# PEER layer of a hybrid trunk: buffer clear moved into the seventh head, v ring begun at free buffers, samples' join in halves

## The reference, cut to what matters

```python
def _peer(x, w_q, k1, k2, u, v):          # 8 heads, 128 x 128 product keys, top 16
    q = (xb @ w_q).reshape(blk, PEER_HEADS, PEER_KEY_DIM)
    s1, s2 = ...                          # q against both halves of the keys
    e = ...                               # the 16 best of the pairs: expert numbers
    gate = jax.nn.softmax(sv, axis=-1)
    act = jax.nn.gelu(jnp.einsum('thkd,td->thk', u[e], xb).astype(jnp.float32), approximate=False)
    return jnp.einsum('thk,thkd->td', (gate * act).astype(x.dtype), v[e])
x = _layernorm(DEEPNORM_ALPHA * x + h, ln_g[l, 0], ln_b[l, 0])   # h: the mixer
f = _peer(x, ...)
x = _layernorm(DEEPNORM_ALPHA * x + f, ln_g[l, 1], ln_b[l, 1])
```

## Time and profile before

| | us |
|---|---|
| three runs, median | 2099.04 (2098.5 to 2102.95) |
| the profiled execution | 2098.57 |
| its span | 2096.8 |

### The profile page before, as it was taken

One profiled execution on the slowest core, in us unless ns is written; L12 is line 12 of the kernel. 1 busy time (PEld: TensorE's weight loads), 2 busy tenths in 40 slices (PEclk: granted clock), 3 DMA queues, 4 the chain that ended last, 5 costly groups with the idle time before them and its releaser, 6 DMA issues.

```text
span 2096.8 us, 21267 instructions
## 1 busy us (share of the span) xinstructions
PE 1222.8 (58%) x6582; PEld 647.7 (31%) x6582; DVE 1186.6 (57%) x3085; ACT 330.7 (16%) x771; POOL 1196.9 (57%) x1104
## 2 busy tenths in 40 slices
PE   6889778910644566575647736664854433333565
PEld 6667535700112222232214314542432100000111
DVE  3555443997667566666441267889457666664101
ACT  3333221110010222232103002321100000000000
POOL 0111002665777777777764554657367777776675
PEclk9899888965775778798669877876978665565578
DMA  8423033877999999999999998888589999998998
GB/s 280 123 81 103 24 131 121 333 261 296 352 420 411 411 354 407 412 409 410 402 421 347 387 369 298 279 296 305 222 347 419 378 377 384 380 383 331 370 419 337
DMA packets 240392, 670.55 MB, mean 320 GB/s; under 512 B 21241, under 2 KB 94482, under 8 KB 236322
## 3 DMA queue, kind: packets, MB, share of 16 engines
q0 software_dynamic: 152064, 553.72, 68.3%
q1 hardware_dynamic: 85922, 98.82, 13.6%
q10 hardware_dynamic: 2304, 16.78, 2.0%
HBM read 663.12 MB, written 6.10 MB: 319 GB/s over the span
## 4 chain that ended last, share of the span: by engine, by line
POOL 31%; PE 18%; DVE 15%; DMA 14%; issue 13%; DVEq 3%; ACT 3%; SPq 1%; ACTq 1%; PEldq 0%; POOLq 0%; PEld 0%
POOL arena L890 31%; DMA arena<-in_peer_v,idxT 8%; DVE arena L1581 7%; DMA arena<-in_peer_u,idx 5%; PE bank L1070 4%; PE bank L664 3%; PE bank L332 2%; PE bank L987 2%; DVEq L470 2%; PE bank L321 1%; PE bank L384 1%; DMA scratch<-in_cache_kv 1%; PE bank L1081 1%; ACT scratch L421 1%; DVE scratch L529 0%
## 5 line engine op out<-in xcount | busy, mean ns | idle before, releaser
L1581 DVE SCALAR_TENSOR_TENSOR arena<-arena,x 128x1024 f32<-128x1024 f32 x512 | 612.6, 1225 | 329.8 <-DMA arena<-in_peer_u,idx 320.9
L890 POOL DMA_INDIRECT arena<-in_peer_u,idx x512 | 583.6, 1140 | 268.6 <-issue 143.6
L890 POOL DMA_INDIRECT arena<-in_peer_v,idxT x512 | 541.1, 1057 | 258.1 <-issue 143.6
L1070 PE MATMUL bank<-arena,wbig 128*32 128x512 f32 x2048 | 378.8, 874 | 502.1 <-DMA arena<-in_peer_v,idxT 493.8
L1070 PEld LDWEIGHTS bank<-arena,wbig 128*32 128x32 f32 x2048 | 77.4, 138 | 736.7 <-issue 727.5
L468 POOL TENSOR_TENSOR scratch<-scratch 128x128 f32<-128x128 f32 x16 | 7.1, 441 | 200.0 <-DVEq L517 200.0
L687 DVE BATCH_NORM_STATS2 stats<-bank 128x6 f32<-128x512 f32 (+1 forms) x24 | 15.5, 685 | 181.4 <-PEq L1084 85.3
L321 PE MATMUL bank<-xT,arena 128*128 128x264 f32 x512 | 115.3, 386 | 0.6 <-DMA arena<-in_hgrn_w_in 0.6
L321 PEld LDWEIGHTS bank<-xT,arena 128*128 128x128 f32 x512 | 96.7, 190 | 16.8 <-issue 0.7
L2069 PE MATMUL bank<-cst,scratch 128*128 128x128 f32 x192 | 48.0, 353 | 53.7 <-DMA scratch<-in_cache_kv 47.5
L987 PE MATMUL bank<-xT,arena 128*128 128x264 f32 (+2 forms) x352 | 71.5, 366 | 2.8 <-ACT xT L639 2.6
(11 more groups left out here) (408 smaller groups left out, 1879.9 us busy)
## 6 DMA issues: line engine op xcount, KB each, us to landing
arena<-in_hgrn_w_in SPq DMA_DIRECT2D x32, 512.0 KB, 6.0
scratch<-in_peer_w_q ACTq DMA_DIRECT2D x14, 1024.0 KB, 8.5
scratch<-in_cache_kv SPq DMA_DIRECT2D x96, 144.0 KB, 8.6
arena<-in_peer_w_q SPq DMA_DIRECT2D x8, 1024.0 KB, 9.0
arena<-in_peer_u,idx POOLq DMA_INDIRECT x512, 7.4
arena<-in_peer_v,idxT POOLq DMA_INDIRECT x512, 7.7
scratch<-in_mla_w_uq SPq DMA_DIRECT2D x2, 2304.0 KB, 13.0
g_all<-in_cache_kv SPq DMA_DIRECT2D x32, 144.0 KB, 12.3
```

The costliest lines, as they stand in the source:

```text
L890: pool.indirect_dma_start(out=dst, out_offset=None, in_=table, in_offset=bass.IndirectOffsetOnAxis(ap=rows, axis=0)).then_inc(done, 16)
L1070: mm = pe.matmul(ybank(t, c, P, 2 * l + 1)[32 * j:32 * j + 32, :], wspread[q % NQ8][:, j, m, :], slot(row[j][0])[:, 512 * c:512 * c + 512] ...
L1581: dve.scalar_tensor_tensor(slot(r), slot(r), 1.0, x[:, t, :], ALU.mult, ALU.mult, accum_out=dots[t][:, TOPK * h + k:TOPK * h + k + 1]).the ...
```

## The change

1. GpSimd clears the weights' buffer at n = 6, k = 8, after `mixed` 2. The wait for the samples' y stands at v row 4, the wait for the stores at v row 0.
2. The v ring of layer 1 begins at slot 12 instead of 8, and `LAG[1]` is 29 instead of 28: a v row follows u by 116 instead of 112.
3. The samples' join uses banks 2 and 3, waits until tile 1's LayerNorm has read them, and is split: between its halves stand tile 1's turn and head 0's projection and score for tile 1 alone. The turned weights of pairs 0 to 2 come ahead of it.
4. The samples' turn and their part of head 0 come after round 0, heads 1 and 2 after rounds 0 and 1, the spread after round 1, and heads 3 to 7 two rounds later than before.
5. VectorE does tile 1's LayerNorm after the last dots of n = 6 and places the weights at once; the samples' LayerNorm and the route of head 8 move into n = 7. ScalarE follows the new order.

```diff
...
                 return bank[5 + c][0:nt, :]
+            if seq == 2 and t == 2:
+                t = 1
...
                 return 6, 7
-            return (0, 1) if t == 1 or (seq, t) in ((4, 2), (5, 2)) else (2, 3)
+            return (0, 1) if t == 1 or (seq, t) == (4, 2) else (2, 3)
...
                 pe.wait_ge(turn_taken, turned((1, 4)[seq], t))
+                if seq and t == 2:
+                    pe.wait_ge(y_free, normed(2, 1))
...
         SAMPLES_AT = 56
-        LAG = (17, 28)
+        LAG = (17, 29)
         STEP0 = (0, 35)
-        SAMPLE_STEP = (34, 35 + 48)
+        SAMPLE_STEP = (34, 35 + 50)
...
             if l:
-                return STEP0[1] + 24 * rest + 3 * h + s
+                return STEP0[1] + 24 * rest + 3 * h + s + (2 if rest and h else 0)
...
             if l:
-                return STEP0[1] + 24 * t + 3 * h + 2
+                return STEP0[1] + 24 * t + 3 * h + 2 + (2 if t and h else 0)
...
             return 6 + 4 * (h - 1) + 2 + t
+
+        def first_sample_step(s):
+
+            return STEP0[1] + 27 + s
...
             if n < WIDE[l]:
-                return RING + n % RING
-            return (RING + (n - WIDE[l]) % (12, 16)[l]) % (2 * RING)
+                return RING + (n + 4 * l) % RING
+            return (RING + 4 * l + (n - WIDE[l]) % (12, 16)[l]) % (2 * RING)
...
                     for k in range(TOPK):
+                        if l and n == 6 and k == 8:
+                            pool.wait_ge(mixed, 2)
+                            pool.memset(wflat[:, 0:4096], 0.0).then_inc(spread_zero, 1)
...
                         place = TOPK * n + k - 4 * LAG[l]
+                        if l and place == 0:
+                            pool.wait_ge(stored, 96)
+                        elif l and place == 4:
+                            pool.wait_ge(y_ready, normed(2, 2))
...
                 pool.memset(zq, 0.0).then_inc(zq_ready, 1)
-                heads(0, HH - 1)
-                pool.wait_ge(y_ready, normed(2, 2))
-                pool.wait_ge(stored, 96)
-                pool.memset(wflat[:, 0:4096], 0.0).then_inc(spread_zero, 1)
-                heads(HH - 1, 2 * HH)
+                heads(0, 2 * HH)
...
             mm.then_inc(rs_ready, 1)
+
+        def pe_first_samples(pe):
+            for s in range(2):
+                b = pe_step(pe, first_sample_step(s))
+                w = wq1_at(HH)
+                for k in range(KO):
+                    mm = pe.matmul(b[:, 0:NS], w[:, k, s * P:(s + 1) * P], xT[:, k, 2 * P:NT], start=(k == 0), stop=(k == KO - 1))
+                mm.then_inc(rs_ready, 1)
...
             pe_join(pe, 1, 1)
-            pe.wait_ge(idxT_ready, 3 * NQ8)
-            pe_join(pe, 1, 2)
-            pe_turn(pe, 5, 1)
-            pe_turn(pe, 5, 2)
-            pe.wait_ge(turn_taken, turned(5, 2))
-            for h in range(3):
-                ask(h, True)
-                pe_score(pe, 1, h, 1)
-            pe_spread_samples(pe, 1)
...
                 turn_weights(pe, 1, q, 4, 0)
+            pe_join_turn(pe, 1, 2)
+            pe_join_half(pe, 1, 2, 0)
+            pe_turn(pe, 5, 1)
+            pe.wait_ge(turn_taken, turned(5, 1))
+            for s in range(2):
+                pe_project(pe, 1, 0, s, P, 2 * P, True)
+            pe_score(pe, 1, 0, 1)
+            pe_join_half(pe, 1, 2, 1)
...
                 add_round(pe, 1, r)
-                h, j = divmod(r + 6, 2)
-                if h < HH:
+                if r == 0:
+                    pe_turn(pe, 5, 2)
+                    pe.wait_ge(turn_taken, turned(5, 2))
+                    pe_first_samples(pe)
+                if r < 2:
+                    ask(r + 1, True)
+                    pe_score(pe, 1, r + 1, 1)
+                if r == 1:
+                    pe_spread_samples(pe, 1)
+                h, j = divmod(r + 4, 2)
+                if 3 <= h < HH:
...
                     turn_weights(pe, 1, q - 1, q, q - 1)
-                if r == 10:
+                if r == 12:
...
                 if h == 0 and s == 0:
-                    act.wait_ge(zq_ready, l + 1)
+                    act.wait_ge(zq_ready, 1)
...
             ins.then_inc(rs_taken, 1)
+
+        def act_first_samples(act):
+            act.wait_ge(zq_ready, 2)
+            for s in range(2):
+                m = first_sample_step(s)
+                act.wait_ge(rs_ready, m + 1)
+                act.activation(zq[:, s, 0, 0:NS], step_bank(m)[:, 0:NS], ACT.Copy).then_inc(rs_taken, 1)
...
             act_turn(act, 4, 2)
-            act_ln(act, 2, (1, 2))
+            act_ln(act, 2, (1,))
             act_turn(act, 5, 1)
+            for s in range(2):
+                act_query(act, 1, 0, s, P, 2 * P, True)
+            act_score(act, 1, 0, 1)
+            act_ln(act, 2, (2,))
             act_turn(act, 5, 2)
-            for h in range(3):
+            act_first_samples(act)
+            act_load_query(act, HH + 2)
+            for h in range(1, 3):
...
                     q = n // 2
-                    own = n + 2 if n < 6 or 9 <= n < 2 * HH - 2 else 8 if n == 7 else None
+                    own = n + 2 if n < 6 or 9 <= n < 2 * HH - 2 else None
...
                     elif n == 7:
-                        for p in range(3):
-                            place_weights(p)
+                        dve_ln(dve, 2, (2,))
+                        route_keys(8)
...
                     dot(n, 2)
-                    if n == 6:
-                        dve_ln(dve, 2, (1,))
+                    if n == 7:
+                        route_pairs(8)
+                        route_experts(8)
...
                         route_experts(own)
-                    if n % 2 and own and n != 7:
+                    if n % 2 and own:
...
                     elif n == 6:
-                        dve_ln(dve, 2, (2,))
+                        dve_ln(dve, 2, (1,))
+                        for p in range(3):
+                            place_weights(p)
...
```

## The result

| | before, us | after, us |
|---|---|---|
| four runs each, median | 2099.92 (2098.5 to 2102.95) | 2132.39 (2129.07 to 2138.92) |
| span of the profiled execution | 2096.8 | 2127.4 |

The account below looks back on a forecast made before the run. No engine is full; holes in GpSimd's order before 1600 us (24.3 and 16.97) are paid in full. Terms -1.9 + 1.0 - 1.0 + 5.0 + 3.7 = +6.8 on 2098.57 or 2099.04 gave 2105.5 us, range 2090 to 2116.

Parts of the forecast that it names:

- (a): GpSimd's clear ahead of u 104: takes 3.67 us beside dots, so u 104 goes out at 1455.7, +2.7.
- (c): Samples' join on TensorE, waiting for banks 2 and 3: ends at 1503.5 (before 1488.3), with 2.5 added for the clock.
- rival 3: TensorE's clock stays at 1.2 GHz through both join halves and the projection: join 8 to 10 later, 2114, chance 0.12.
- (d): GpSimd during the join: v 4 waits until 1503.8, a hole of 18.6 us; the hole at v 8 closes.
- (f): VectorE's weigh(3) waits for pair 3's gelu behind head 4's score: u 140 at 1581.4, hole some 25 us, 1.9 gain left.
- (g): After u 140: +1.0 at u 144, -1.0 for pace to u 255, +5.0 for lagged gathers, +3.7 for the samples' repack.
- (e): u 128, waiting for head 8's route: out at 1525.4, 26.1 us earlier, with u 123 landing in 7.
- Rival 1: The change works and weigh(3) is not waited for: -17.4, 2081; chance 0.14 with its milder forms.

Follow-up runs that it names:

- e1: The changed kernel with ScalarE's gelu of pair 3 moved right behind the samples' spread; 2104.44 us, ratio 1.0011 to the kernel before.
- e7: The kernel before with only the scores of heads 3 to 7 and the samples two rounds later; 2120.26 us, ratio 1.0068.
- e4: e3 with the samples' repack after round 33 instead of 34; 2094.38 us, ratio 0.9965 to the kernel before.
- e5: e4 with SyncE's two 512 KB loads of LayerNorm weights waiting for the samples' score; 2091.14 us, ratio 0.9932 to the kernel before.
- e2: The changed kernel with ScalarE's gelu of pair 4 moved ahead of the samples' score; 2123.33 us, ratio 1.0108 to the kernel before.
- e3: The changed kernel with both gelus, of pairs 3 and 4, moved earlier; 2098.54 us, ratio 0.9973 to the kernel before.
- e10: e5 with the samples' join in one piece again; 2085.61 us, ratio 0.9916 to the kernel before.
- e6: The kernel before with all of e4's moves (both gelus and the repack); 2112.22 us, ratio 1.0042.
- e8: e4 with the lag at 28 and the repack at round 34 again; 2099.87 us, ratio 0.9962 to the kernel before.

## Why the prediction was right in sign and wrong in size

**Right.** (a) The clear took 3.53 us beside VectorE's back-to-back dots; in before, where VectorE was at the samples' LayerNorm on 8 partitions, it took 3.51. GpSimd came free for it at 1453.12, not 1451.7, so u 104 went out at 1456.81 (forecast 1455.7). The Trainium skill (SBUF — State Buffer, section "SBUF: two separate sides") has a GpSimd operation that only writes stay clear of a VectorE operation with two SBUF inputs, as the dots are; the trace agrees, 3.53 beside the dots. (c) TensorE's timeline, the waiting half of the join, tile 1's turn and projection, the second half, seed and round 0:

```profile
1477.69 1.86 PE L665 MATMUL bank<-x,cst 8*8 8x512 f32 x2 [5.05 <-DVE x L700]
1479.49 6.48 PE L668 MATMUL bank<-wbig,xT 128*8 128x512 f32 x8
1485.81 3.60 PE L668 MATMUL bank<-arena,xT 128*8 128x512 f32 x8
1489.33 1.09 PE L633 MATMUL bank<-cst,x 128*128 128x128 f32 x8
1491.16 3.84 PE L998 MATMUL bank<-xT,scratch 128*128 128x128 f32 x32 [0.74 <-ACT xT L641]
...
1500.46 3.60 PE L668 MATMUL bank<-arena,xT 128*8 128x512 f32 x8
1503.99 1.98 PE L1045 MATMUL bank<-x,cst 128*128 128x512 f32 x4
1505.90 1.92 PE L1089 MATMUL bank<-arena,wbig 128*32 128x512 f32 x16
```

The join ended at 1504.0 (forecast 1503.5) and v 4 went out at 1504.33 (1503.8). The clock after the pause cost 6.48 - 3.60 = 2.9, and some of the first row's 1.86 (1.02 at full clock): 3.7 where 2.5 stood. The granted clock was 0.50 from 1476 to 1484 and 1.00 from 1488 to 1512: full speed again within the half, so rival 3 didn't come. (d) The hole at v 4 was 14.37, not 18.6, since the gathers ahead of it took longer beside the dots (1.99 each for the last three); its end, which counts, was right. No hole at v 8, v 12 or v 16. (f) The mechanism, its place, its releaser and its size: 26.82 against some 25, an idle stretch of 32.35 against about 30. e1 shows that it costs 24.6, and e7 that the later scores alone, without the rest of the change, make such a wait, of 14.93. (g) The repack's step, 3.7 forecast, 3.94 in e4.

**Term (e), 6.0 too small.** u 128 went out at 1531.40, not 1525.4. I let u 123 land in 7 us. It went out at 1510.96 (forecast 1510), and its dot ran at 1523.56, 12.6 later. The row was there in before; the 17 gathers that before issued from 1488 to 1520, with SyncE's two loads beside them as well (1492.90 and 1493.29):

```profile
DMA to landing us min/median/max: 7.1/12.0/14.5
```

After, 1500 to 1535:

```profile
DMA to landing us min/median/max: 9.4/12.6/14.0
```

I took a value without other loads beside it for gathers that share the DMA engines with these loads (1508.62 and 1509.00 in after). With 12.0 the sum would have had +5. It is the loads and not the restart: in e5, without them, u 123 landed in 6.1, and u 128 stood 302.2 behind u 0, 26.2 less than in before, where 26.1 were forecast.

**Term (f), 2.3 too small.** From u 128 to u 140 58.3 us passed, forecast 56.0: v 23 went out 30.53 after u 128 (29.2 forecast) and round 5 began 10.31 after that (9.5). With term (e): u 140 at 1589.69 and not 1581.4. Step (f) said that 1.9 of the gain are left; in truth 6.4 were lost.

**Step (g), the one that failed.** "The change touches it little" was written of u 140 to u 255. The stretch was 14.8 longer and not equal. e2 shows that 12.4 of that are the gelu of pair 4; the other 2.4 are within what single executions differ by. I followed the two-round shift of `divmod` to one gelu and not to the second one, and passed over `if r == 12` though it is in the diff; the argument of (f), applied to it, gives v 51 behind u 167 and the wait at u 172. The tail, +8.7 forecast, was +9.4.

Together: 6.0 + 2.3 + 14.8 + 0.7 = 23.8, which is the span's +30.6 less the +6.8 of the sum. Rival 1 (-17.4, 2081, chance 0.14) took the wait for the gelu out and left everything else. e3 is that kernel, without pair 4's wait too, and its ratio of 0.9973 is 6 us: rival 1's price was wrong as well. Only with the earlier repack, the later loads and the join in one piece besides is it reached (e10, 0.9916, 18 us).

## What to carry to other kernels

When work in one engine's hand-written order is moved by some rounds, list everything that stands behind it on every engine that takes its result, to the end of the shift and not to the first victim; here two 0.23 us gelus behind moved scores cost 37 us, some six times what the rest of the change gained (e3, 6 us). For each, count in the bottleneck's own units (which gather must land, and how many gathers stand between it and the one that will wait): a shift by 8 gathers turned a wait that cost nothing (e5, 8.81 us on VectorE, no hole) into a hole of 12. And the same early place isn't good in each kernel: where its inputs come late, it blocks what stands behind (e6).

## What was not expected of the hardware

Two plain loads of 512 KB lengthened the landings of the gathers beside them, u 123's from 6.1 us (e5) to 12.6 (after). v 4 to v 7, the 7 gathers right behind the gate, landed in 11.1 us (median) in after and 12.5 in e4, with the loads issued some 4 us after v 4; without them in 7.4 (e5) and 6.5 (e10), against 6.2 in the steady queue.

A gather queue that had run dry restarted with short landings. In e8 GpSimd had stood idle for 21.27 us, the DMA engines moved nothing from 1496 to 1512, SyncE's loads came only at 1530.50, and v 4 to v 7 landed like this:

```profile
DMA to landing us min/median/max: 6.0/6.4/6.4
```

Behind v 7 the landings grew without SyncE's loads too: the six gathers from v 8 on took 11.2 (median) in e5, where ScalarE's load of query weights (1 MB) went out at 1518.46, and 8.9 in e8, where none went out before 1538.88. That the query weights are the difference is an assumption; no kernel moved them alone.
